# A two-block sequence model on one core: the position bias loaded in its final order, small matrix products before the first tokens arrive, the last product in column parts

## What is computed

```python
# first block, each layer
proj = x @ w_in[l]                       # split into 12 groups of columns
s_w = einsum(q, k) * scale + head_bias(dist)     # head_bias: rb[t5_bucket(dist)], 8 heads
p = masked_softmax(s, dist >= 0); o = p @ v      # the same bias for the selected and window branches
...
# end of the second block, each layer
x = x + ffn(rms_norm(x))
gate = sigmoid(rms_norm(x) @ w_ple_gate)         # 1024 x 1024
x = x + gate * e                                  # e: a projected and normed embedding
```

## Time and profile before

| | |
|---|---|
| runs | 1690.7, 1691.69, 1694.94 us |
| the profiled execution | span 1691.7 us |
| PE busy | 1628.0 us (96%) |
| DVE, ACT, POOL busy | 1167.2, 918.8, 445.8 us |
| moved by DMA | 288.74 MB, mean 171 GB/s |

### The profile page before, as it was taken

One profiled execution on the slowest core, in us unless ns is written; L12 is line 12 of the kernel. 1 busy time (PEld: TensorE's weight loads), 2 busy tenths in 40 slices (PEclk: granted clock), 3 DMA queues, 4 the chain that ended last, 5 costly groups with the idle time before them and its releaser, 6 DMA issues.

```text
span 1691.7 us, 30151 instructions
## 1 busy us (share of the span) xinstructions
PE 1628.0 (96%) x11354; PEld 1484.1 (88%) x11354; DVE 1167.2 (69%) x1601; ACT 918.8 (54%) x1576; POOL 445.8 (26%) x184
## 2 busy tenths in 40 slices
PE   8889999999989999999999999999999999999997
PEld 7878799988987899978899989999788999899996
DVE  5787754558777644476784877776758756777767
ACT  5664544446745544465555664454765555554545
POOL 2212222222222222233511122222235311223222
PEclk9999999999999999999999999999999999999999
DMA  9532466556423655546423456666464333466653
GB/s 334 164 119 90 154 207 198 191 171 204 155 81 131 219 196 193 189 150 210 151 88 111 133 187 198 212 213 194 154 220 150 101 112 124 169 212 207 217 193 125
DMA packets 82563, 288.74 MB, mean 171 GB/s; under 512 B 9051, under 2 KB 11908, under 8 KB 81924
## 3 DMA queue, kind: packets, MB, share of 16 engines
q1 hardware_dynamic: 77352, 272.58, 48.6%
q10 hardware_dynamic: 5084, 14.37, 2.6%
HBM read 284.81 MB, written 2.11 MB: 170 GB/s over the span
## 4 chain that ended last, share of the span: by engine, by line
PE 64%; DVE 6%; ACT 2%; issue 2%; DVEq 0%; ACTq 0%
PE bank L727 30%; PE bank L744 26%; PE bank L1301 2%; DVE w_lo L693 1%; PE bank L1282 1%; PE bank L1273 1%; PE bank L1261 1%; PE bank L772 1%; PE bank L781 1%; PE bank L1314 0%; ACT w_hi L689 0%; DVE small L2555 0%; DVE z L2511 0%; PE bank L917 0%; PE bank L925 0%
## 5 line engine op out<-in xcount | busy, mean ns | idle before, releaser
L693 POOL TENSOR_TENSOR w_lo<-raw,w_hi 128x1024 fp32r<-128x1024 f32 x146 | 382.7, 2621 | 1140.7 <-ACT w_hi L689 1140.7
L693 DVE TENSOR_TENSOR w_lo<-raw,w_hi 128x1024 fp32r<-128x1024 f32 x364 | 557.7, 1557 | 145.8 <-ACT w_hi L689 144.0
L689 ACT ACTIVATE w_hi<-raw 128x1024 fp32r<-128x1024 f32 x510 | 518.1, 1051 | 85.3 <-PE bank L744 44.1
L727 PE MATMUL bank<-x_t_hi,w_hi 128*128 128x256 f32 x1984 | 318.8, 283 | 1.8 <-ACT p_t L556 1.1
L727 PE MATMUL bank<-x_t_hi,w_lo 128*128 128x256 f32 x1984 | 309.5, 278 | 0.0
L727 PE MATMUL bank<-x_t_lo,w_hi 128*128 128x256 f32 x1984 | 308.5, 278 | 0.0
L727 PEld LDWEIGHTS bank<-x_t_hi,w_hi 128*128 128x128 f32 x1984 | 272.0, 190 | 13.7 <-issue 5.2
L727 PEld LDWEIGHTS bank<-x_t_hi,w_lo 128*128 128x128 f32 x1984 | 266.3, 190 | 0.0
L727 PEld LDWEIGHTS bank<-x_t_lo,w_hi 128*128 128x128 f32 x1984 | 264.6, 189 | 0.0
L744 PE MATMUL bank<-w_hi,x_t_hi 128*128 128x512 f32 (+3 forms) x448 | 133.8, 381 | 6.9 <-issue 3.4
L744 PE MATMUL bank<-w_hi,x_t_lo 128*128 128x512 f32 (+3 forms) x448 | 132.0, 378 | 1.7 <-DVE x_t_lo L1975 1.7
(11 more groups left out here) (391 smaller groups left out, 2112.0 us busy)
## 6 DMA issues: line engine op xcount, KB each, us to landing
raw<-stream SPq DMA_DIRECT2D x511, 512.0 KB, 4.4
rows<-rows ACTq DMA_DIRECT2D x4, 1024.0 KB, 4.4
gain<-rows ACTq DMA_DIRECT2D x8, 512.0 KB, 4.0
hv_p<-hv_dram ACTq DMA_DIRECT2D x14, 256.0 KB
x<-x_in SPq DMA_DIRECT2D x2, 512.0 KB, 5.0
bias_r<-rev_dram SPq DMA_DIRECT2D x1, 1024.0 KB, 7.0
hv_dram<-hv ACTq DMA_DIRECT2D x2, 512.0 KB, 7.5
y_out<-x SPq DMA_DIRECT2D x2, 512.0 KB, 2.7
```

Of the source, the lines that this page charges most:

```text
L689: self.eng.activation(w_hi[:, i, :], raw[:, i, :], ACT.Copy).then_inc(hi_done.sem, 1)
L693: self.eng.tensor_tensor(w_lo[:, i, :], raw[:, i, :], w_hi[:, i, :].bitcast(F32), ALU.subtract).then_inc((lo_pool if self.part == "pool" e ...
L727: mm = pe.matmul(target, a[:, i, w0 + kt * P:w0 + (kt + 1) * P], b[:, k0 + kt, :], start=kt + k == 0, stop=k == 2 and kt == kts - 1)
```

## The change

1. **Bias.** `flip`, `bias_r` and the six products are gone. SP now stores `rev` 128 times over for each head (`rev_dram` is 8 x 128 x 384, 1.5 MB), and loads `bias` from it with a row step of 383 elements, so that each row starts one element further back in its own copy. DVE waits for that load before `bias_c`; PE and ACT no longer wait for any of it.
2. **SP's order.** After the store come units 7 and 8, then the wait for the store, the two bias loads, units 9 to 13, and only then param2, positions, freq and band.
3. **Start on PE.** Six float32 products of `ones` by `ones` (128 x 128) go ahead of the first transposes and four behind the product for `rev`; their result is not read. The first four units are multiplied unit by unit in turns over the two halves of the tokens, and hi by hi starts when `w_hi` is there, before `w_lo`. DVE copies `rev` before its first split; ACT and DVE take the halves of the token tiles between the splits.
4. **End.** In the last layer the columns of the second 128 tokens go in parts of 512, 256 and 256, each with its own signal, sigmoid, multiply, add and store. The splits of the seven unused units are gone, and SP no longer loads all of them.

```diff
-        rev_dram = nc.dram_tensor("rev_dram", [8, 384], F32, kind="Internal").ap()
+        rev_dram = nc.dram_tensor("rev_dram", [NH, P, 384], F32, kind="Internal").ap()
...
-            sp.dma_start(flip[:], flip_in).then_inc(flip_in_sem, 16)
...
             sp.wait_ge(setup_dve, 1)
-            sp.dma_start(rev_dram, rev[:]).then_inc(rev_stored, 16)
+            sp.dma_start(rev_dram, rev[:].unsqueeze(1).broadcast_to([NH, P, 384])).then_inc(rev_stored, 16)
+            unit_after(0)
+            unit_after(1)
             sp.wait_ge(rev_stored, 16)
-            for (c0, n, first) in ((0, P, P), (P, S, 0)):
-                sp.dma_start(bias_r[:, :, c0:c0 + n], bass.AP(rev_dram.tensor, first, [[1, P], [384, NH], [1, n]])
+            for (c0, n, first) in ((0, P, 2 * P - 1), (P, S, P - 1)):
+                sp.dma_start(bias[:, :, c0:c0 + n], bass.AP(rev_dram.tensor, first, [[383, P], [P * 384, NH], [1, n]])
                              ).then_inc(bias_loaded, 16)
+            for i in range(2, RING):
+                unit_after(i)
...
-            with sp.Fori(1, (total_units + RING) // RING) as r:
+            with sp.Fori(2, total_units // RING) as r:
...
-            for t in range(T):
-                sp.wait_ge(x_ready.sem, LAST_X - 1 + t)
-                sp.dma_start(out[t * P:(t + 1) * P], x[:, t, :]).then_inc(stored, 16)
+            for n, (t, c0, cn) in enumerate(PARTS):
+                sp.wait_ge(*c["ple_done"](last, n + 1))
+                sp.dma_start(out[t * P:(t + 1) * P, c0:c0 + cn], x[:, t, c0:c0 + cn]).then_inc(stored, 16)
...
+            def keep_busy(n):
+                for _ in range(n):
+                    pe.matmul(bank[3][:, 0:P], ones[:], ones[:], start=True, stop=True)
...
                 if at.index == 0:
+                    pe.wait_ge(setup_pool, 1)
+                    keep_busy(6)
                     pe.wait_ge(ident_in_sem, 16)
...
+                    keep_busy(4)
+                    pe.wait_ge(*banks.free(at, "hi"))
+                    for n, t in ((0, 0), (1, 0), (0, 1), (1, 1), (2, 0), (2, 1), (3, 0), (3, 1)):
+                        if (n, t) == (1, 0):
+                            x_turned(1)
...
-                if at.index == 0:
-                    bias_turned()
                 nsa_tick(0)
...
+                        for part in parts:
+                            for k in range(4, 8):
+                                end = token_major(at, uid[f"pg{k}"], [[], [part]], x_t_hi, x_t_lo, k, 1, D,
+                                                  False, k == 7, [1], False)
+                            end[0].then_inc(pg_part, 1)
...
-                split.upto(N2 + 3)
+                split.upto(N2 + 3 if at.reg + 1 < L else N2)
...
-                    flat = bias[:].rearrange("p h n -> p (h n)")
-                    for n in range(0, 6, 2):
-                        dve.wait_ge(*banks.full(at, f"flip{n}"))
-                        dve.tensor_copy(flat[:, 512 * n:512 * n + 512], bank[banks.bank(at, f"flip{n}")][:]
-                                        ).then_inc(*banks.frees(at, f"flip{n}"))
-                    for n in range(6):
-                        dve.wait_ge(*banks.read(at, f"flip{n}"))
+                    dve.wait_ge(bias_loaded, 32)
```

More of the change, by code:

```diff
@@ L524, in params, with last_parts @@
             return params_loaded(at, 16)
+        def last_parts(at):
+            b = [bank[2], bank[3], bank[banks.bank(at, "zt00")]]
+            return [(b[n][:, 0:width], c0, width) for n, (_, c0, width) in enumerate(PARTS[2:])]
         def x_begun(at, t):
@@ L832, in first_block, with x_turned @@
                 uid = place(UNITS1)
+                def x_turned(t):
+                    tile_turned(at, "xt", t, x, lambda h: pe.wait_ge(*x_ready(at, 2 * t + h - 3)))
                 if at.index == 0:
+                    pe.wait_ge(setup_pool, 1)
+                    keep_busy(6)
                     pe.wait_ge(ident_in_sem, 16)
[L835 to L847, removed]
@@ L1384, in second_block @@
                     pe.wait_ge(*banks.free(at, f"pg{t}"))
+                    if t and parts:
+                        pe.wait_ge(*banks.read(at, "zt00"))
                     rounded, split = tile_parts(at, "zt", t, 16)
-                    token_split(at, [uid[f"pg{k}"] for k in range(4)], t, wide(0), x_t_hi, x_t_lo, 0, 1, D, True, False,
+                    token_split(at, [uid[f"pg{k}"] for k in range(4)], t, gated, x_t_hi, x_t_lo, 0, 1, D, True, False,
                                 lambda n: rounded(0), lambda n: split(0))
@@ L1389, in second_block @@
                     pe.wait_ge(*banks.read(at, f"zt{t}1"))
-                    token_split(at, [uid[f"pg{k}"] for k in range(4, 8)], t, wide(0), x_t_hi, x_t_lo, 4, 1, D, False, True
-                                ).then_inc(*banks.fills(at, f"pg{t}"))
+                    if t == 0 or not parts:
+                        token_split(at, [uid[f"pg{k}"] for k in range(4, 8)], t, gated, x_t_hi, x_t_lo, 4, 1, D, False, True
+                                    ).then_inc(*banks.fills(at, f"pg{t}"))
+                    else:
+                        for part in parts:
[3 more added lines that the diff above has]
+                            end[0].then_inc(pg_part, 1)
             for l in range(L):
@@ L1923, in second_block @@
                 else:
-                    embedding_gate(1)
-                    split.ahead(N2 - 1)
+                    for n in range(2, len(PARTS)):
+                        _, c0, n_c = PARTS[n]
+                        act.wait_ge(pg_part, n - 1)
+                        act.wait_ge(*c["ple_done"](at, min(n - 1, 2)))
+                        act.activation(ple[:, c0 // 512, c0 % 512:c0 % 512 + n_c], last_parts(at)[n - 2][0], ACT.Sigmoid
+                                       ).then_inc(c["ple_sig"].sem, 1)
                 step.end("act_step")
@@ L2734, in second_block @@
                 else:
-                    embedding_added(2)
-                    embedding_added(3)
-                    split.ahead(N2 - 1)
-                step.end("dve_step")
+                    for n in range(2, len(PARTS)):
+                        _, c0, n_c = PARTS[n]
+                        dve.wait_ge(*c["ple_sig"](at, n + 1))
+                        v, g = x[:, 1, c0:c0 + n_c], ple[:, c0 // 512, c0 % 512:c0 % 512 + n_c]
+                        step(dve.tensor_tensor(g, g, e[:, 1, c0:c0 + n_c], ALU.mult))
+                        dve.tensor_tensor(v, v, g, ALU.add).then_inc(c["ple_done"].sem, 1)
+                if at.reg + 1 < L:
+                    step.end("dve_step")
             for l in range(L):
```

112 lines of the change are left out of this document (66 added, 46 removed).

## The result

The changed kernel took **1710.58 us** (median of 6 runs, 1705.73 to 1711.85). Six runs of the kernel before beside it had a median of 1694.17 us (1690.7 to 1695.92). The ratio is 1.0094, with an interval of 1.0082 to 1.0107: slower by 16.4 us (13.9 to 18.1), where 7 us faster was forecast. The profiled execution took 1711.85 us, and its span is 1709.7 us.

The account below looks back on a forecast made before the run. PE, busy 1628.0 of 1691.7 us, was taken as the bound, with time to win where it idles, runs slowly or has ended. 1691.7 - 4.5 (end) - 3.6 (start) + 1.0 (clock) = 1684.6 us; range 1681 to 1708.

Parts of the forecast that it names:

- The store: Storing `rev` 128 times over: 1.57 MB at half the full DMA rate, 7.9 us, landing at 23.3 us.
- The rival of the slow store: Eight partitions read through two paths of 25 GB/s: store 31.5 us, result 1708.2; no gain from 15.0 us; chance 0.31.
- my bound from rows 8: DMA rate of the store: 3.9 us at the full 399 GB/s, 63 us at eight partitions' share of it.
- The gain behind the store: From unit 10 (36.1 us) over `nq0` to scores at 44.4, first bias addition about 49, transposes 52.4: gain 3.6 us.
- The clock: Start on PE: ten dummy products raise the clock between 8 and 12 us, putting PE 2 us ahead, hidden behind ACT.
- The statement that this changes nothing in the sum: Start on PE: dummies not raising the clock leave the sum unchanged, ACT being the bound at 44.4; no chance of its own.
- the clock in PE's idle stretch: PE idle from 37.9 to 44.4 us: the clock may fall there; 0 to 2 us allowed, 1.0 us taken as cost.
- The end: Last layer: unused splits removed and column parts, so the end comes 3.8 us after the last product; gain 4.5 us.
- the wrong-if clause: First block: forecast wrong if the scores come later than 55 us, or if PE stands before `nq0`.

Follow-up runs that it names:

- e2: The changed kernel with the eight source rows on partitions 0, 4 to 28 instead of side by side; 1690.45 us, ratio 0.9974 to the kernel before.
- e4: The changed kernel with the old way of the bias and SP's old order, keeping the new start and end; 1689.89 us, ratio 0.9972.
- e5: e1 with DVE's chain for `lbc` moved from ahead of the first bias addition to behind the third pair of softmax items; 1684.16 us, ratio 0.9934.
- e8: The changed kernel with the eight source rows two partitions apart (0, 2 to 14); 1694.2 us in one run, the kernel before beside it 1694.94.
- e9: The changed kernel with the eight source rows sixteen partitions apart (0, 16 to 112); 1694.49 us in one run, the kernel before beside it 1698.21.
- e10: The changed kernel with units 7 and 8 issued ahead of the store instead of behind it; 1713.77 us in one run, the kernel before beside it 1698.21.
- e6: e1 without the ten small products at the start; 1687.38 us, ratio 0.9951 to the kernel before.
- e7: e1 with the order of the start as before, so also without the ten small products; 1687.24 us, ratio 0.9953 to the kernel before.
- e3: The kernel before with the new end alone (column parts, no unused splits or loads); 1691.7 us, ratio 0.9983.
- e1: The changed kernel with the bias row made on all 128 partitions and stored from there, 8 copies by each; 1686.78 us, ratio 0.9957 to the kernel before.

## Why the prediction was wrong

**The store: the step that failed.** I took 7.9 us for it, since "eight source rows can keep eight of sixteen DMA engines at the pace that rows 8 show". It took 30.8 us. The half about the engines was right (share 0.45; with eight paths, in e2, 9.0 us); the half about their pace was not: each packet took 220 ns instead of 65 because all eight rows lie behind two paths: with nothing else changed in the store, the rows four partitions apart have 65 again (e2). The rival of the slow store had this mechanism and 31.5 us, and its result, 1708.2, was 16.5 us above the profile of before; the measured difference is 16.4 (in part by luck, see below). I had put its chance at 0.31 because no row of the trace showed a packet slowed by its partition. But no row could: the kernel before reads many bytes out of few partitions nowhere. That a trace doesn't show a limit was no evidence against it, and the Trainium skill's figure (SBUF — State Buffer, Door 1: The DMA port swizzle) of 27.6 GB/s for partitions 0 to 3 should have weighed more than my bound from rows 8: the runs show 25 to 26 GB/s for each path, and 27 to 28 by the packets' own times (four of 1536 bytes in 220 ns, two in 113).

**The Trainium skill's rule on the outermost dimension** (DMA: Bandwidth & Descriptors, Rules for kernel authors), at most as many engines as that dimension's size, here eight, agrees with the traces: with eight rows the share stayed at 0.45 to 0.47, some 7 engines, in three kernels. It alone would have given about e2's time.

**The gain behind the store: a second term that failed.** I priced the way from unit 10 over ACT's copy of `nq0` to the scores, and let DVE add the first bias at "about 49". In e2 unit 10 was rounded at 35.37 (I had 36.1) and the scores came at 43.77 (44.4). That the chain is right to 0.7 us is luck, from two errors that offset each other: the bias load was issued at 24.92 (I had the store landed at 23.3), and from there unit 10 took 10.5 us and not 12.8. But the first `z` came at 51.13, not 49, and the 3.6 us of gain shrank to 0.3. What I missed stands in DVE's own queue: its `lbc` chain waits for ACT, which is late with unit 10, and after it come three splits, the copies and `blocks_hl`, 8.65 us in one piece (63.03 to 71.68). Removing the six products took DVE's copies and waits for them out of this queue, 19.31 to 15.8 us, which is 3.5 us; unit 10, 4 us later by my own forecast, would have used them all up. By e2's rows, 1.1 us earlier for a store of 7.9 us, the first `z` would have come at 50.0, a gain of 1.4 us (an estimate) where the sum had 3.6. It also follows that the start breaks even with unit 10 rounded at 35.6 us (51.42 less 15.8), e2's store of 9 us; with the 2.9 us of the end the whole change does so at 38.5, a store of some 12 us, where the rival gave 15.

**The rival's own steps** were less right than its sum. Its store landed at 47 (the bias load was issued at 45.97), but its scores were at 68 and came at 64.31, so 20 us late by its sum and 16.3 by the trace: the store landed 1 us sooner, and from the bias load's issue to unit 10 it took 9.9 us for the 12.8 of the sum. The 4 us so won were lost again behind the scores, on DVE. That the rival's total fits is luck to this extent; its mechanism is what the runs show. Units 7 and 8 were not issued at 10.9 and 12.8 as in the sum but from 10.77 and 22.2 on, and waited for the store either way.

**The clock.** I expected the rise between 8 and 12 us; the pace of the upper level came at 14.7 us (14.66 before). PE took 0.70 us for a pair at 14.70 and 1.20 us at 10.45, with the granted clock at 1.00 in both. PE was not ahead by 2 us but level: the first projection stands at 24.40 (24.32 before). That is not what the small products do in every execution: in e2, e4, e5, e8, e9 and e10, which have them too, the upper pace was first seen between 4.8 and 7.1 us, and the first projection stood at 21.4 to 22.7. The statement that this changes nothing in the sum held in the timed runs of e6 and e7, within their intervals. For the clock in PE's idle stretch I had allowed 1.0 us. It was low from 35.2 to 55.7 us; the products in there (49.70 on) cost PE time, but it waits again before the scores, 3.49 us, so nothing of it is in the result. Two short stretches at the lower level, 3.4 us each, came behind it (65.9, 79.5); the second, with PE busy, costs half its length, 1.7 us. PE's lag was 20.3 us at the second scores and 22.9 us at its last product (1706.29 and 1683.40), from which the end took 4.9: the 18.0 us of the span. Where the rest of these 2.6 us arose was not pursued.

**The end.** 3.8 us from the last product to the end were forecast, 3.4 measured; the gain of 4.5 us was 4.9 in the profile, and 2.9 (1.4 to 4.4) in the timed runs of e3. PE's last stage took 16.90 us in column parts, 16.75 in the kernel before. That the timed gain is smaller was not pursued; it is not settled whether the 2 us are the runs' scatter. The 3.8 us counted 2.4 for the last store, which took 1.7.

**What held.** No L864 in the trace; the bias load (landed about 7 us after its issue) held nobody; none of PE's long waits is put down to the parameters, issued 33 us later (17.44 and 50.37); and the wrong-if clause was met on both counts: scores later than 55 us and PE standing before `nq0`.

## What to carry to other kernels

Before a small tensor is broadcast or stored many times over by DMA, count two things: how many rows the DMA's outermost dimension has, and how many SBUF paths the source partitions reach; when a product can make 128 copies of the rows for the same time as 8, let it. A transfer that goes ahead of the weight stream on the same queues is paid by the first unit behind it, so price it from both ends and find the unit at which the saving is used up. And follow each consumer's queue to its own next product: the engine that was waiting before (PE for the bias) is not the one that is late after (DVE).

## What the runs showed of the hardware that was not expected

- A 1536-byte packet out of SBUF took 65 ns (median) with the rows on eight or more paths, 108 to 113 ns on four, 220 ns on two, the paths counted by the Trainium skill's table (SBUF — State Buffer, Door 1: The DMA port swizzle); the busy share of the DMA engines hides this, since a slowed packet counts as busy.
- Rows 16 partitions apart were no faster than rows two apart (14.9 and 14.0 us), both slower than rows four apart (9.0 us).
- Behind the slow store SP's issue of one 512 KB load took 11.4 us in itself (8.6 in e8, 7.2 in e2, 2.0 in e1; 0.33 in e10, ahead of the store), and the load landed at 47.2 us, 36.4 us after its issue began. What holds the issue was not pursued.
- With the ten small products the upper pace was first seen early in six of eight profiles: at 5.6 us (e2), 6.1 (e4), 7.1 (e8), 6.9 (e9), 6.7 (e10) and 4.8 (e5, where it fell back at 8.2 and rose again at 11.6), but at 14.7 in the changed kernel and 14.1 in e1. Without them it came at 14.6 (before), 13.0 (e3), 16.3 (e6) and 15.3 (e7), never early. So they look like a chance of an early rise and no guarantee: in the changed kernel PE worked from 1.86 us on with no stop above 0.4 us, and kept the lower pace until 14.7. With one profile for each kernel, and e1 and e6 the only pair that differs in these products alone, the cause is not shown. None of the results follows these times.
